# Two attention units ahead of the latent products, one-row products in pairs, the heads' Sqrt behind the last Exp

## The chip, the core and the metric

The program runs on one core of one Trainium2 chip, as one launch. The core has five engines that run their own instruction streams and meet at semaphores: TensorE (PE, matrix products and transposes into eight PSUM banks), VectorE (DVE), ScalarE (ACT), GpSimd (POOL) and SyncE (SP, which here issues the weight loads). The metric is device time in microseconds (us) of one execution.

## The reference, cut to what matters

Two transformer blocks run one after the other on 256 tokens of width 1024, in float32. The first block has attention over 512 keys (256 context, 256 own), of two kinds with four heads each, and a mixture of 32 experts with four chosen per token; the second has a pooling mixer, windowed attention and a wide feed-forward part. The change touches the attention of the first block:

```
mod  = silu(c) @ w_ada + b_ada          # 6 vectors of 1024; sa, sca before attention, ga, sf, scf, gf behind it
q    = rmsnorm(cq, q_norm_w) @ w_uq     # latent queries:  q_nope, q_rope per head
kv   = rmsnorm(ckv, kv_norm_w) @ w_ukv  # latent keys and values: k_nope, mv per head
diff:  p = softmax(q1 k1) - lam * softmax(q2 k2);  o = p @ dv          # 4 heads
mla:   p = softmax(q_nope k_nope + q_rope k_rope); o = p @ mv          # 4 heads
o_diff = rmsnorm(o_diff, subln_w) * 0.8        # per head: needs a square root
x_new  = x + ga * (concat(o_diff, o_mla) @ w_out)
```

## The kernel before, in words

**Weights.** All weights go through a ring of 12 slots of 1 MB in SBUF. SP issues the chunks in a fixed order (`FRONT`: ada0, w_in, w_uq, w_ukv, ada1, ada2, w_out; then 16 pairs of experts in blocks of two slots; then the second block). SP waits with a chunk until PE has counted up `ring_freed` to the chunk's place minus 11, so a slot is loaded again when the products that read it are done.

**Order of the work.** Nothing is scheduled by a program: every engine's stream is written out by hand, and the order of attention comes from one function, `skewed_order`, that PE, ACT and DVE all loop over. There are 16 units, each a head and a half of the queries (128 of them): units 0 to 7 are the differential heads (kind "d", two score tiles each, s{u}_0 and s{u}_1), units 8 to 15 the latent heads (kind "m", one score tile). A unit has four steps, which are skewed by one unit each: *score* (PE multiplies queries and keys, DVE takes the negated maximum of each row, ACT takes Exp with its sum), *mix* (DVE: reciprocal, and for "d" the difference of both softmaxes into `prob`, two buffers), *turn* (PE transposes the probabilities, tile pT{u}, ACT copies them to `probT`) and *value* (PE multiplies with the values, tile av{u}, DVE scales it into `o`).

**Banks.** Every PSUM tile has a name in `FRONT_TILES`, and the tiles take the eight banks in turn, in the list's order. `claim` makes PE wait until the bank's last tile was read, `take` makes a reader wait until the tile is full, `wait_read` waits for a tile's reading. The list has to follow the order in which PE fills the tiles.

**Ahead of attention.** Behind the input projection, PE transposes keys and queries (dkT, dqT) and the latents (cqT, ckvT, krT), multiplies the latent queries with w_uq (qrope, qnope0, qnope1), then w_ukv with the latents: knope0 to knope3 (copied by ACT into knT) and mv0 to mv3 (copied by DVE), and transposes the rotated queries (qrT). These nine tiles are called the latent products here. Only units 8 to 15 read them.

**Inside attention.** Behind value 3 stand the second and third third of the modulation: ada1 and ada2, of 32 products of 32 columns by 512 each; then eight products bc0 to bc7 whose stationary side is one row of `ones`, which spread the modulation's rows over all partitions (`bc`). DVE adds the bias to ada1 and ada2 and copies the eight tiles. Behind value 5 PE transposes 16 pieces of one row of `bc` into *columns*, which POOL later multiplies with the router's weights. Behind value 9 DVE takes eight sums of squares of the heads (`ms_done`) and ACT their root (`root_done`); behind value 12 DVE scales the heads (`sub_done`). PE waits for `sub_done` before mixT0, the first transpose behind attention, and the products with w_out follow.

ACT holds one table of functions at a time. Exp and Sqrt are in different tables (a Copy or a Square needs no change); the compiler puts ACT_TABLE_LOAD ahead of the first of a kind.

Of the kernel before, what the change touches and what calls it, by code (L numbers as in the profile page):

```python
# [9 lines left out]
ALU = mybir.AluOpType  # L10
# [3 lines left out]
P = 128  # L14
# [93 lines left out]
for _c, _n in CHUNK.items():  # L108
# [9 lines left out]
    + ["qrope", "qnope0", "qnope1"] + [f"knope{h}" for h in range(H)] + [f"mv{t}" for t in range(4)] + ["qrT"]  # L118
)
UNITS = [("d", h, t) for h in range(H) for t in range(NT)] + [("m", h, t) for h in range(H) for t in range(NT)]  # L120
# [21 lines left out]

def skewed_order(n_units):

    order = []
    for i in range(n_units + 3):
        for what, u in (("score", i), ("mix", i - 1), ("turn", i - 2), ("value", i - 3)):
            if 0 <= u < n_units:
                order.append((what, u))
    return order  # L150


for _what, _u in skewed_order(len(UNITS)):
    if _what == "score":
        FRONT_TILES += [f"s{_u}_{c}" for c in range(2 if UNITS[_u][0] == "d" else 1)]
    elif _what != "mix":
        FRONT_TILES.append(f"{'pT' if _what == 'turn' else 'av'}{_u}")
    if _what == "value" and _u == 3:
        FRONT_TILES += ["ada1", "ada2"] + [f"bc{n}" for n in range(8)]
    if _what == "value" and _u == 5:  # L160
        FRONT_TILES.append("columns")
# [56 lines left out]
def build(nc, a, out):  # L218
    with ExitStack() as ctx:
# [726 lines left out]
        def _(act):  # L946
# [72 lines left out]
            act.wait_ge(full("proj3_2"), use("proj3_2") + 1)  # L1019
            for h in range(H):  # L1020
                b = take(act, f"knope{h}")
                step(act.activation(knT[:, h, :], b[:], ACT.Copy), tile=f"knope{h}")

            for what, u in skewed_order(len(UNITS)):
                kind, h, t = UNITS[u]
                if what == "score":
# [13 lines left out]
                elif what == "value" and u == 5:  # L1040
# [172 lines left out]
        def _(dve):  # L1213
# [143 lines left out]
            for t in range(4):  # L1357
                b = take(dve, f"mv{t}")
                step(V.tensor_copy(mv[:, t, :], b[:]), tile=f"mv{t}")
            b = take(dve, "qrT")  # L1360
            step(V.tensor_scalar(qrT, b[:].rearrange("p (j t) -> p j t", j=2), MLA_SCALE, None, ALU.mult), tile="qrT")

            for what, u in skewed_order(len(UNITS)):
                kind, h, t = UNITS[u]
                if what == "score":
# [32 lines left out]
                if what == "value" and u == 12:  # L1398
# [261 lines left out]
        def _(pe):  # L1660
# [143 lines left out]
            nk = ("w_ukv", 0)  # L1804
            ring_wait(pe, nk)
            wkv = slot(nk)[:, 0:1024].rearrange("p (h c) -> p h c", h=H)
            wait_read(pe, "ckvT")
            for h in range(H):
                b = claim(pe, f"knope{h}")
                mm(b[:], wkv[:, h, 0:NOPE], ckvT, True, True).then_inc(full(f"knope{h}"), 1)  # L1810
            for t in range(4):
                b = claim(pe, f"mv{t}")
                m = mm(b[:], ckvT[:, t * P:(t + 1) * P], wkv[:, :, NOPE:2 * NOPE], True, True)
                m.then_inc(full(f"mv{t}"), 1)
            pe.wait_ge(full("mv3"), use("mv3") + 1)
            pe.sem_inc(freed, 1)
            wait_read(pe, "qrope")
            b = claim(pe, "qrT")
            for j in range(2):
                for t in range(NT):  # L1820
# [485 lines left out]
```

## Time and profile before

| | |
|---|---|
| time, 3 runs | 1486.64 us median (1486.0 to 1487.38) |
| profiled execution | 1488.94 us, span 1487.1 us |
| busy, of the span | PE 1377.2 us (93%), PE weight loads 741.3 (50%), DVE 505.0 (34%), ACT 309.9 (21%), POOL 46.9 (3%) |
| DMA moved | 500.07 MB, mean 336 GB/s; GB/s by slice of 37.2 us: 389 120 3 387 398 77 157, then 425 to 429, in the slice before 1153 us 423, then 365 266 108 |

The span is the stretch from the first to the last instruction that the profiler records; the execution's own time is 1.8 us more. A busy share is a mean over stages with different limits, so the stretch in question has to be looked at by itself. In the timelines of one engine the bracket behind a row gives how long the engine had been idle and what ended that. A float32 product shows as two records.

### The profile page before, as it was taken

The page shows a single profiled execution, that of the slowest core. Times are in us where ns is not written, and L with a number is a line of the kernel's source. Part 1 is how long each engine was busy: PE and PEld are TensorE (multiplying, and loading weights), DVE is VectorE, ACT ScalarE, POOL GpSimd, SP SyncE. Part 2 cuts the span into 40 slices and gives each one's busy share as a digit, 9 for nine tenths or more (in the row PEclk, how much of TensorE's full clock was granted, in tenths as well). Part 3 has the DMA queues.
Part 4 walks back from the last instruction along what each step waited for, and adds up shares of the span by engine and source line. Part 5 has one row for each costly group of instructions (what it writes and reads, how often), then busy time and mean ns, then how long its engine had stood idle before and what let it go on. Part 6 is the DMA issues. An engine that isn't in the chain of part 4 may idle for free.

```text
span 1487.1 us, 17478 instructions
## 1 busy us (share of the span) xinstructions
PE 1377.2 (93%) x6850; PEld 741.3 (50%) x6850; DVE 505.0 (34%) x896; ACT 309.9 (21%) x451; POOL 46.9 (3%) x74
## 2 busy tenths in 40 slices
PE   5998999999989889899898898898989899999998
PEld 2785455433334324333334343343333487889987
DVE  2746434313113112121131131111311347755566
ACT  3605233201101101011011010010100254544451
POOL 2000000200000000000000000000000201000000
PEclk9999999999999999999999999999999999999999
DMA  9309925999999999999999999999999973565530
GB/s 389 120 3 387 398 77 157 425 429 428 428 428 429 428 429 427 429 428 429 427 429 429 428 428 428 429 428 429 427 428 423 365 266 108 173 196 181 187 142 29
DMA packets 62766, 500.07 MB, mean 336 GB/s; under 512 B 5288, under 2 KB 21960, under 8 KB 34240
## 3 DMA queue, kind: packets, MB, share of 16 engines
q1 hardware_dynamic: 60480, 492.85, 80.4%
q0 software_dynamic: 2032, 6.05, 1.4%
q8 instruction: 31, 0.51, 0.1%
q10 hardware_dynamic: 208, 0.54, 0.1%
q14 instruction: 15, 0.12, 0.0%
HBM read 498.37 MB, written 1.05 MB: 336 GB/s over the span
## 4 chain that ended last, share of the span: by engine, by line
PE 63%; DMA 23%; DVE 9%; issue 3%; SPq 1%; ACT 1%; DVEq 0%; ACTq 0%; PEldq 0%
PE bank L1662 27%; DMA ring<-in_w 20%; PE bank L671 15%; PE bank L724 15%; DMA ring<-in_w_in 2%; PE bank L746 2%; DVE dk L814 1%; DVE mrows L808 1%; DVE dk L810 1%; DVE mrows L818 1%; PE bank L682 1%; PE bank L696 1%; PE bank L734 1%; SPq L546 1%; PE bank L1849 0%
## 5 line engine op out<-in xcount | busy, mean ns | idle before, releaser
L671 PE MATMUL bank<-ring,xn 128*64 128x512 f32 x2048 | 467.9, 610 | 62.2 <-DMA ring<-in_w 62.1
L671 PEld LDWEIGHTS bank<-ring,xn 128*64 128x64 f32 x2048 | 161.1, 140 | 358.0 <-issue 357.2
L724 PE MATMUL bank<-ring,dq 128*64 128x512 f32 x1024 | 226.8, 595 | 0.1
L760 ACT ACTIVATE sq<-mrows 128x512 f32<-128x512 f32 x32 | 20.1, 630 | 802.8 <-DVE mrows L808 802.8
L808 DVE TENSOR_SCALAR mrows<-bank 128x512 f32<-128x512 f32 x32 | 22.0, 687 | 467.3 <-PE bank L671 467.3
L724 PEld LDWEIGHTS bank<-ring,dq 128*64 128x64 f32 x1024 | 71.0, 137 | 136.5 <-issue 136.1
L827 DVE TENSOR_TENSOR dk<-bank,bc 128x512 f32<-128x512 f32 x32 | 22.1, 691 | 236.0 <-PE bank L724 236.0
L501 DVE TENSOR_TENSOR w_lo<-ring,w_hi 128x2048 fp32r<-128x2048 f32 x34 | 77.7, 2291 | 32.8 <-ACT w_hi L496 32.8
L1662 PE MATMUL bank<-x_hi,w_hi 128*128 128x256 f32 x256 | 72.4, 283 | 0.8 <-DVE h_lo L1540 0.8
L1662 PE MATMUL bank<-x_hi,w_lo 128*128 128x256 f32 x256 | 72.4, 283 | 0.0
L1662 PE MATMUL bank<-h_lo,w_hi 128*128 128x256 f32 x256 | 72.4, 283 | 0.0
L496 ACT ACTIVATE w_hi<-ring 128x2048 fp32r<-128x2048 f32 x36 | 68.4, 1907 | 17.2 <-PE bank L1662 17.0
L653 PEld LDWEIGHTS bank<-xn 128*128 128x128 f32 x512 | 58.4, 192 | 14.0 <-issue 14.0
L746 PE MATMUL bank<-dk,xn 128*128 128x512 f32 x128 | 62.3, 620 | 0.0
L653 PE MATMUL bank<-xn 128*128 128x128 f32 x512 | 61.7, 278 | 0.7 <-DVE xn L789 0.7
L1662 PE MATMUL bank<-w_hi,wide_hi 128*128 128x512 f32 x128 | 50.5, 395 | 0.1
L1662 PE MATMUL bank<-w_lo,wide_hi 128*128 128x512 f32 x128 | 50.5, 395 | 0.0
L1662 PEld LDWEIGHTS bank<-x_hi,w_hi 128*128 128x128 f32 x256 | 49.0, 191 | 2.3 <-issue 1.6
L834 DVE TENSOR_TENSOR xc<-xc,bank 128x512 f32<-128x512 f32 x64 | 44.0, 687 | 17.0 <-PE bank L746 17.0
L1662 PEld LDWEIGHTS bank<-h_lo,w_hi 128*128 128x128 f32 x256 | 49.1, 192 | 0.6
L1662 PEld LDWEIGHTS bank<-x_hi,w_lo 128*128 128x128 f32 x256 | 49.0, 192 | 0.0
L1662 PE MATMUL bank<-w_lo,x_hi 128*128 128x512 f32 (+1 forms) x136 | 47.2, 366 | 0.0
(435 smaller groups left out, 1522.1 us busy)
## 6 DMA issues: line engine op xcount, KB each, us to landing
ring<-in_w SPq DMA_DIRECT2D x186, 2048.0 KB, 17.2
ring<-in_w_ff SPq DMA_DIRECT2D x32, 1024.0 KB, 5.5
ring<-in_w_ada SPq DMA_DIRECT2D x24, 1024.0 KB, 16.0
ring<-in_w SPq DMA_DIRECT2D x12, 1024.0 KB, 18.0
ring<-in_w_out SPq DMA_DIRECT2D x8, 1024.0 KB, 10.5
ring<-in_w_in SPq DMA_DIRECT2D x8, 992.0 KB, 26.4
ring<-in_w_in SPq DMA_DIRECT2D x8, 640.0 KB, 15.0
ring<-in_w_ple_gate SPq DMA_DIRECT2D x4, 1024.0 KB, 4.8
```

Source lines behind the costliest of these rows:

```text
L496: act.activation(hi_of(n).bitcast(F32R), slot(chunk)[:, cols], ACT.Copy).then_inc(sem("w_rounded"), 1)
L501: eng.tensor_tensor(w_lo[:, SLOT_OF[chunk], cols].bitcast(F32R), slot(chunk)[:, cols], hi_of(n), ALU.subtract)\
L546: sp.dma_start(dst, src).then_inc(sem(f"landed{SLOT_OF[chunk]}"), 16)
L653: m = pe.matmul(banks[GATHER_BANKS[k // 4]][:, k % 4 * P:(k % 4 + 1) * P], hf[:, t, k * P:(k + 1) * P], sel[:, t, :], start=t == 0, stop=t ...
L671: m = pe.matmul(banks[bank_no][mine(i), :], gathered[:, k, mine(i)], rows_of(at + i, 2)[:, k % 2, q * 512:(q + 1) * 512], start=k == 0, st ...
L724: m = pe.matmul(banks[OUT_BANKS[c]][mine(i), :], actT[:, k, mine(i)], rows_of(8 + 2 * j + i, 4)[:, r, c * 512:(c + 1) * 512], start=k == 0 ...
L746: pe.matmul(banks[MIX_BANKS[c]][:], selgT[:, t * P:(t + 1) * P], out2[:, c * 512:(c + 1) * 512], start=True, stop=True, skip_group_check=T ...
L760: act.activation(sg[:, cols], gs[:, cols], ACT.Sigmoid, scale=ALPHA).then_inc(moe("sigmoid", which), 1)
L808: dve.tensor_scalar(gs[:, cols], banks[GATE_BANKS[half]][:], LIMIT, None, ALU.min)\
L827: dve.tensor_tensor(out2[:, cols], banks[OUT_BANKS[c]][:], gf[:, cols], ALU.mult)\
L834: dve.tensor_tensor(x2[:, t, cols], x2[:, t, cols], banks[MIX_BANKS[c]][:], ALU.add)\
L1662: return pe.matmul(out_, lhsT, rhs, start=first, stop=last, skip_group_check=True)
```

## The change

Three things are moved; no arithmetic of the reference is changed.

1. `skewed_order` starts with score 0, score 1, mix 0, mix 1 and an entry *latent*, at which all three engines do the latent products; then it goes on as before from unit 2. One Exp of a single column is added on ACT between dqT1 and qnope0 (its result is read by nobody), so that the Exp table is loaded there.
2. ada2 goes from behind value 3 to behind value 4, and the eight one-row products go two at a time behind values 5, 6, 7 and 8; columns goes from behind value 5 to behind value 9.
3. ACT's Sqrt goes from behind value 9 to behind value 13, and DVE's scaling of the heads from behind value 12 to behind value 13.

```diff
+LATENT_TILES = [f"knope{h}" for h in range(H)] + [f"mv{t}" for t in range(4)] + ["qrT"]
...
+ADA_AFTER = {3: 1, 4: 2}
+SPREAD_AFTER = {5: (0, 1), 6: (2, 3), 7: (4, 5), 8: (6, 7)}
+
+
 def skewed_order(n_units):
 
-    order = []
-    for i in range(n_units + 3):
+    order = [("score", 0), ("score", 1), ("mix", 0), ("mix", 1), ("latent", 0)]
+    for i in range(2, n_units + 3):
         for what, u in (("score", i), ("mix", i - 1), ("turn", i - 2), ("value", i - 3)):
-            if 0 <= u < n_units:
+            if (2 if what == "mix" else 0) <= u < n_units:
                 order.append((what, u))
...
# ACT
+            step(act.activation(stat[:, 57:58], lam[:, 0:1], ACT.Exp))
             for j in range(2):
                 b = take(act, f"qnope{j}")
...
-                elif what == "value" and u == 9:
+                elif what == "value" and u == 13:
 
                     act.wait_ge(sem("ms_done"), 3)
                     step(act.activation(stat[:, 48:56], stat[:, 40:48], ACT.Sqrt), "root_done")
...
# DVE
-                if what == "value" and u == 12:
+                if what == "value" and u == 13:
                     dve.wait_ge(sem("root_done"), 3)
...
-                if what == "value" and u == 3:
-
+                if what == "value" and u in ADA_AFTER:
+                    i = ADA_AFTER[u]
                     dve.wait_ge(sem("bada_in"), 64)
-                    for i in (1, 2):
-                        b = take(dve, f"ada{i}")
-                        step(V.tensor_tensor(mrows[:, i, :], b[:], mrows[:, i, :], ALU.add), tile=f"ada{i}")
-                    for n in range(8):
+                    b = take(dve, f"ada{i}")
+                    step(V.tensor_tensor(mrows[:, i, :], b[:], mrows[:, i, :], ALU.add), tile=f"ada{i}")
+                if what == "value" and u in SPREAD_AFTER:
+                    for n in SPREAD_AFTER[u]:
                         b = take(dve, f"bc{n}")
...
# PE
-                if what == "value" and u == 3:
-                    ada(1)
-                    ada(2)
-
-                    wait_read(pe, "ada1")
-                    wait_read(pe, "ada2")
-                    for n, (third, q) in enumerate(((1, 0), (1, 1), (1, 2), (1, 3), (2, 0), (2, 1), (2, 2), (2, 3))):
+                if what == "value" and u in ADA_AFTER:
+                    ada(ADA_AFTER[u])
+                if what == "value" and u in SPREAD_AFTER:
+                    for n in SPREAD_AFTER[u]:
+                        third, q = 1 + n // 4, n % 4
+                        wait_read(pe, f"ada{third}")
                         b = claim(pe, f"bc{n}")
                         mm(b[:], ones[32 * q:32 * q + 1, :], mrows[32 * q:32 * q + 1, third, :], True, True)\
                             .then_inc(full(f"bc{n}"), 1)
-                if what == "value" and u == 5:
+                if what == "value" and u == 9:
                     wait_read(pe, "bc5")
```

PE's order behind the latent queries, before. `cq,ring` is qnope, `ckv,ring` knope, `ring,ckv` mv, L1821 qrT, `xc,dqT` the scores of a "d" unit, L1849 a turn, `dv,dq` a value:

```order
L1662 MATMUL bank<-cq,ring 128x256 x8
L1662 MATMUL bank<-ckv,ring 128x512 x4
L1662 MATMUL bank<-ring,ckv 128x512 x4
L1821 MATMUL bank<-ident,xn 128x128 x4
L1662 MATMUL bank<-xc,dqT 128x512 x6
L1849 MATMUL bank<-ident,xn 128x128 x4
L1662 MATMUL bank<-xc,dqT 128x512 x2
L1849 MATMUL bank<-ident,xn 128x128 x4
L1662 MATMUL bank<-dv,dq 128x128 x4
```

and after (L1833 is qrT, L1862 a turn):

```order
L1672 MATMUL bank<-cq,ring 128x256 x8
L1672 MATMUL bank<-xc,dqT 128x512 x4
L1672 MATMUL bank<-ckv,ring 128x512 x4
L1672 MATMUL bank<-ring,ckv 128x512 x4
L1833 MATMUL bank<-ident,xn 128x128 x4
L1672 MATMUL bank<-xc,dqT 128x512 x2
L1862 MATMUL bank<-ident,xn 128x128 x4
L1672 MATMUL bank<-xc,dqT 128x512 x2
L1862 MATMUL bank<-ident,xn 128x128 x4
L1672 MATMUL bank<-dv,dq 128x128 x4
```

The scores of units 0 and 1 (four rows) now stand ahead of the nine latent tiles, and those of unit 2 stay behind them.

PE's order from the first modulation product, before. `ring,cT` is ada1 and ada2, `mrows,ones` the one-row products, `hT,xn` with `kr,xn` the score of an "m" unit, L1874 the columns:

```order
L1662 MATMUL bank<-ring,cT 32x512 x64
L1662 MATMUL bank<-mrows,ones 128x512 x8
L1662 MATMUL bank<-xc,dqT 128x512 x2
L1849 MATMUL bank<-ident,xn 128x128 x4
L1662 MATMUL bank<-dv,dq 128x128 x4
L1662 MATMUL bank<-hT,xn 128x512
L1662 MATMUL bank<-kr,xn 128x512
L1849 MATMUL bank<-ident,xn 128x128 x4
L1662 MATMUL bank<-dv,dq 128x128 x4
L1874 MATMUL bank<-ident,bc 128x1 x16
L1662 MATMUL bank<-hT,xn 128x512
L1662 MATMUL bank<-kr,xn 128x512
```

and after:

```order
L1672 MATMUL bank<-ring,cT 32x512 x32
L1672 MATMUL bank<-xc,dqT 128x512 x2
L1862 MATMUL bank<-ident,xn 128x128 x4
L1672 MATMUL bank<-dv,dq 128x128 x4
L1672 MATMUL bank<-ring,cT 32x512 x32
L1672 MATMUL bank<-hT,xn 128x512
L1672 MATMUL bank<-kr,xn 128x512
L1862 MATMUL bank<-ident,xn 128x128 x4
L1672 MATMUL bank<-dv,dq 128x128 x4
L1672 MATMUL bank<-mrows,ones 128x512 x2
L1672 MATMUL bank<-hT,xn 128x512
L1672 MATMUL bank<-kr,xn 128x512
```

ada2 stands one unit later than ada1, and the one-row products come in pairs, the first behind the turn and value that follow the first "m" score; the columns stand further on, behind value 9.

ACT's order around the head's Sqrt, before. `xn,psum_sum` is an Exp, `dq` a copy of transposed probabilities, `stat` the Sqrt:

```order
L1033 ACTIVATE xn,psum_sum<-bank,psum_sum 128x512
L1039 ACTIVATE dq<-bank 128x512
L1046 ACT_TABLE_LOAD
L1046 ACTIVATE stat<-stat 128x8
L1033 ACT_TABLE_LOAD
L1033 ACTIVATE xn,psum_sum<-bank,psum_sum 128x512
L1039 ACTIVATE dq<-bank 128x512
L1033 ACTIVATE xn,psum_sum<-bank,psum_sum 128x512
L1039 ACTIVATE dq<-bank 128x512
L1033 ACTIVATE xn,psum_sum<-bank,psum_sum 128x512
L1039 ACTIVATE dq<-bank 128x512 x3
```

and after (the same names):

```order
L1043 ACTIVATE xn,psum_sum<-bank,psum_sum 128x512
L1049 ACTIVATE dq<-bank 128x512
L1043 ACTIVATE xn,psum_sum<-bank,psum_sum 128x512
L1049 ACTIVATE dq<-bank 128x512
L1043 ACTIVATE xn,psum_sum<-bank,psum_sum 128x512
L1049 ACTIVATE dq<-bank 128x512 x2
L1056 ACT_TABLE_LOAD
L1056 ACTIVATE stat<-stat 128x8
L1049 ACTIVATE dq<-bank 128x512
L1059 ACTIVATE hT<-bank 128x512 x2
```

The Sqrt is now behind the last Exp and behind the copy for unit 14, with one copy (unit 15) behind it, and no Exp table is loaded behind it.

## Rows read from the trace of the kernel before

**Rows 1.** Page of the profile, the chain that ended last, by engine.
```profile
PE 63%; DMA 23%; DVE 9%; issue 3%; SPq 1%; ACT 1%; DVEq 0%; ACTq 0%; PEldq 0%
```

**Rows 2.** Busy time by stage, all engines; the first line names the columns.
```profile
core 0: us, PE busy (x) PEld busy (x) DVE busy (x) ACT busy (x) POOL busy (x), PEclk, DMA share, GB/s
192.00:200.00 8.00, 6.20 (x31) 3.36 (x28) 3.38 (x13) 5.53 (x9) 0.00 (x0) 1.00 0.01 4
254.00:256.00 2.00, 2.00 (x12) 0.64 (x10) 0.00 (x0) 0.00 (x0) 0.00 (x0) 1.00 0.00 0
400.00:600.00 200.00, 184.12 (x848) 72.56 (x848) 43.13 (x86) 18.20 (x29) 0.00 (x0) 0.99 1.01 428
```

**Rows 3.** Page, DMA issues: KB of each, us from issue to landing.
```profile
ring<-in_w SPq DMA_DIRECT2D x186, 2048.0 KB, 17.2
```

**Rows 4.** Timeline of PE: start us, us, engine line operation, [idle before].
```profile
120.21 3.67 PE L1662 MATMUL bank<-ckv,ring 128*128 128x512 f32 x8 [0.30 <-PE bank L1662]
...
128.18 2.85 PE L1662 MATMUL bank<-xc,dqT 64*128 64x512 f32 x12
134.47 1.12 PE L1849 MATMUL bank<-ident,xn 128*128 128x128 f32 x4 [3.45 <-DVE xn L1386]
```

**Rows 5.** Timeline of DVE, same stretch.
```profile
129.40 2.87 DVE L1368 TENSOR_REDUCE psum_sum<-bank 128x1 f32<-128x512 f32 x4 [0.36 <-PE bank L1662]
...
133.66 0.75 DVE L1386 SCALAR_TENSOR_TENSOR xn<-xn,psum_sum 128x512 f32<-128x512 f32 x1
...
140.77 1.42 DVE L1368 TENSOR_REDUCE psum_sum<-bank 128x1 f32<-128x512 f32 x2
```

**Rows 6.** Timeline of ACT, same stretch.
```profile
118.67 0.60 ACT L1017 ACTIVATE xn<-bank 128x512 f32<-128x512 f32 x1 [4.18 <-PE bank L1662]
...
130.19 1.28 ACT L1033 ACT_TABLE_LOAD   x1 [5.62 <-DVE psum_sum L1368]
131.49 0.69 ACT L1033 ACTIVATE xn<-bank,psum_sum 128x512 f32<-128x512 f32 x1
```

**Rows 7.** Timeline of PE, the modulation products and what follows.
```profile
148.08 7.07 PE L1662 MATMUL bank<-ring,cT 128*32 128x512 f32 x64
155.49 7.07 PE L1662 MATMUL bank<-ring,cT 128*32 128x512 f32 x64 [0.33 <-PE bank L1662]
163.48 2.29 PE L1662 MATMUL bank<-mrows,ones 1*128 1x512 f32 x16 [0.93 <-DVE mrows L1411]
165.70 2.52 PE L1662 MATMUL bank<-xc,dqT 64*128 64x512 f32 x4
...
170.77 1.59 PE L1662 MATMUL bank<-hT,xn 128*128 128x512 f32 x2
...
174.82 1.15 PE L1874 MATMUL bank<-ident,bc 1*128 1x1 f32 x16
```

**Rows 8.** Busy time and granted clock (PEclk) in two stretches.
```profile
166.00:168.00 2.00, 2.00 (x4) 0.65 (x3) 1.90 (x4) 0.00 (x0) 0.00 (x0) 0.50 1.05 418
174.00:176.00 2.00, 2.00 (x25) 1.86 (x24) 1.81 (x5) 1.38 (x3) 1.48 (x7) 1.00 1.04 442
```

**Rows 9.** Timeline of PE, second half of attention.
```profile
179.39 1.02 PE L1662 MATMUL bank<-hT,xn 128*128 128x512 f32 x2
...
192.96 1.02 PE L1662 MATMUL bank<-hT,xn 128*128 128x512 f32 x2
...
198.42 1.02 PE L1662 MATMUL bank<-hT,xn 128*128 128x512 f32 x2
...
206.96 1.91 PE L1888 MATMUL bank<-ident,dk 128*128 128x128 f32 x16
```

**Rows 10.** Timelines of ACT and of DVE, same stretch.
```profile
193.15 1.28 ACT L1046 ACT_TABLE_LOAD   x1 [2.52 <-DVE stat L1397]
...
194.67 1.28 ACT L1033 ACT_TABLE_LOAD   x1
...
202.72 1.42 DVE L1404 TENSOR_TENSOR dk<-dk,stat 128x512 f32<-128x512 f32 x2
```

More of the change, by code:

```diff
@@ L155 @@
         FRONT_TILES += [f"s{_u}_{c}" for c in range(2 if UNITS[_u][0] == "d" else 1)]
+    elif _what == "latent":
+        FRONT_TILES += LATENT_TILES
     elif _what != "mix":
         FRONT_TILES.append(f"{'pT' if _what == 'turn' else 'av'}{_u}")
-    if _what == "value" and _u == 3:
-        FRONT_TILES += ["ada1", "ada2"] + [f"bc{n}" for n in range(8)]
-    if _what == "value" and _u == 5:
+    if _what == "value" and _u in ADA_AFTER:
+        FRONT_TILES.append(f"ada{ADA_AFTER[_u]}")
+    if _what == "value":
+        FRONT_TILES += [f"bc{n}" for n in SPREAD_AFTER.get(_u, ())]
+    if _what == "value" and _u == 9:
         FRONT_TILES.append("columns")
@@ L1018, in _ @@
                                     ACT.Copy, scale=MLA_SCALE), tile=f"qnope{j}")
[L1019 to L1022, printed above, removed]
             for what, u in skewed_order(len(UNITS)):
                 kind, h, t = UNITS[u]
-                if what == "score":
+                if what == "latent":
+                    act.wait_ge(full("proj3_2"), use("proj3_2") + 1)
+                    for n in range(H):
+                        b = take(act, f"knope{n}")
+                        step(act.activation(knT[:, n, :], b[:], ACT.Copy), tile=f"knope{n}")
+                elif what == "score":
                     for c in range(2 if kind == "d" else 1):
@@ L1803, in _, with latent @@
             pe.sem_inc(freed, 1)
[L1804 to L1820, printed above, removed]
-                    m = pe.transpose(b[:, j * T + t * P:j * T + (t + 1) * P], qr[:, t, j * P:(j + 1) * P], ident[:])
-            m.then_inc(full("qrT"), 1)
+            def latent():
+                nk = ("w_ukv", 0)
+                ring_wait(pe, nk)
+                wkv = slot(nk)[:, 0:1024].rearrange("p (h c) -> p h c", h=H)
+                wait_read(pe, "ckvT")
+                for h in range(H):
+                    b = claim(pe, f"knope{h}")
+                    mm(b[:], wkv[:, h, 0:NOPE], ckvT, True, True).then_inc(full(f"knope{h}"), 1)
+                for t in range(4):
+                    b = claim(pe, f"mv{t}")
+                    m = mm(b[:], ckvT[:, t * P:(t + 1) * P], wkv[:, :, NOPE:2 * NOPE], True, True)
+                    m.then_inc(full(f"mv{t}"), 1)
+                pe.wait_ge(full("mv3"), use("mv3") + 1)
+                pe.sem_inc(freed, 1)
+                wait_read(pe, "qrope")
+                b = claim(pe, "qrT")
+                for j in range(2):
+                    for t in range(NT):
+                        m = pe.transpose(b[:, j * T + t * P:j * T + (t + 1) * P], qr[:, t, j * P:(j + 1) * P], ident[:])
+                m.then_inc(full("qrT"), 1)
             for what, u in skewed_order(len(UNITS)):
                 kind, h, t = UNITS[u]
-                if what == "score" and kind == "d":
+                if what == "latent":
+                    latent()
+                elif what == "score" and kind == "d":
                     if u == 0:
```

17 lines of the change are left out of this document (9 added, 8 removed).

## The prediction

> **What bounds the kernel now.** I read the chain that ended last first [rows 1]: TensorE (PE) carries 63% of the span and DMA 23%, so no single engine sets the end everywhere. Next the busy time by stage [rows 2]. From 400 to 600 us the DMA share is 1.01 at 428 GB/s while PE is busy for 184.12 of 200 us: in the mixture-of-experts stage the weight stream is at its limit. In 192:200 and 254:256 the DMA share is 0.01 and 0.00: twice before that stage the stream stands still, because every ring slot is full and PE has not given one back. So the stream's last start, a little before 260 us, is set by PE, and behind it everything has a fixed length. A check on that: the experts' weights are 186 issues of 2048 KB plus twelve halves [rows 3], 402.7 MB, of which 12 slots (12.6 MB) are there when the stream starts; 390 MB at 428 GB/s are 911 us, which from about 259 us ends at about 1170 us, just where the page's GB/s line falls off (423 in the slice that ends at 1153 us, 365 in the next). Each microsecond taken from the front should therefore come off the end, one for one.
>
> All of the change lies in the front, between 113 and 209 us. There PE is the engine on the chain, with holes. The timeline of PE [rows 4, 7, 9] shows these: PE runs the latent products at 120.21, then the scores of three units at 128.18, and then stands idle for 3.45 us until 134.47, when turn 0 may start; its clock is at the lower level (1.2 GHz) behind that. It runs the two modulation products (ada1, ada2) at 148.08 and 155.49 with nothing of attention between them, then eight one-row products at 163.48, and behind these its granted clock is 0.50 (166:168, [rows 8]): the scores of unit 7, two products of 64x512, take 2.52 us where their like takes 1.1. In the second half of attention a unit's rows come every 3.39 us (179.39 to 192.96 are four periods, [rows 9]), PE-bound; then one period is 5.46 (192.96 to 198.42), where ACT loads the Sqrt table and the Exp table again [rows 10].
>
> **Term 1: two units ahead of the latent products.** PE's order changes as the first ordered rows show. Work is the same; what counts is what runs beside what.
> - PE: the scores of units 0 and 1 start at 120.21 instead of 128.18 [rows 4]. Six such products took 2.85 us, so four take 1.9. The latents follow at 122.1 and last as before, 128.18 - 120.21 = 8.0 us, to 130.1.
> - DVE: the first maximum came 1.2 us behind the first score (129.40, [rows 5]); now 121.4. Four maxima take 2.87 us: 124.2.
> - ACT: the Exp table load (1.28 us, [rows 6]) stood behind the first maximum, on the path. It moves in front of qnope0, where ACT had been idle for 4.18 us (the row at 118.67): hidden. The first Exp starts at about 122.15, each takes 0.69 + 0.1 (read of the sum, partly overlapped), four until 125.4. DVE mixes unit 0 from 124.25 to 125.4 (0.75 us for the large one, 1.2 with the two small ones, [rows 5]) and unit 1 to 126.7, all beside PE's latents.
> - Price: DVE's four mv copies and qrT stand before the maxima of unit 2, ACT's four knope copies before its Exp. qrT is full at about 130.2, DVE has copied it (0.7, a pass as wide as a maximum, [rows 5]) at 130.95, and the scores of unit 2 (130.1 to 131.2) are full at 131.2: no wait. The banks that the latents claim are drained 2 us or more before they are needed.
> - Then: turn 0 at 131.1 (its mix is long done), maxima of unit 2 to 132.7, Exp 132.1 to 133.7, copy of pT0 (0.6) to 134.3, value 0 from 134.4 to 135.4, scores of unit 4 to 136.4, and its maximum at 136.5. It stood at 140.77 [rows 5]. From there DVE's cycle of 3.08 us a unit is unchanged. I take 4.2 us: ada1 starts at 143.9, not at 148.08.
> Bounds: not below 1 (the table load alone is 1.28), not above 8.0, the whole latent block. A hole of 1.3 us is left on PE (133.1 to 134.4), shorter than the 1.8 that 192:200 has at full clock [rows 2].
>
> **Term 2: ada2 behind value 4, the one-row products two at a time.** Before, from ada1's start to the first score of unit 8: 170.77 - 148.08 = 22.7 us [rows 7]. Now: ada1 7.1, the wait for its completion 0.3, scores, turn and value of unit-slot 7 at full clock 2.55, ada2 7.1, wait 0.3: 17.35 us. The eight one-row products come later, 0.285 each (2.29 for eight, [rows 7]), 2.3 in all. Saved: 22.7 - 17.35 - 2.3 = 3.1 us. This is the half clock and the wait of 0.93 before the one-row products (163.48 row). DVE's copies of the spread rows (eight, 0.7 each) no longer stand in one block before the maxima of unit 7; two of them a unit make DVE 1.4 + 1.25 = 2.7 us of a PE period of 3.39 + 0.57 = 3.96, so they hide. Bounds: 0 (each pair costs a bank wait of the size of the 0.93) to 5.4 (they vanish in PE's shadow altogether).
> The ring: ada2 is freed later relative to ada1, but starts at 153.8 instead of 155.5, and its chunks land earlier, since ada1 frees the first of them at 144.8, before the stream has run dry. Four blocks of the experts are loaded by about 186 and wait for PE anyway (192:200 has no DMA, [rows 2]), so no load gets late. The load of router_w waits for the second half of unit 7 and comes earlier; the transposed columns (16 one-column transposes, 1.15 us) come later, at about 181, with the small GpSimd products behind them done some 25 us before PE asks.
>
> **Term 3: units 8 to 15.** Before: from unit 8's first score to that of unit 15, 198.42 - 170.77 = 27.65 us [rows 7, 9]. Now seven periods of 3.39 are 23.7, plus 1.1 for the columns: 24.8 (the 2.3 for the one-row products are in term 2). Saved: 2.8, of which 2.07 is the Sqrt hole (5.46 - 3.39) and the rest what was left of the half clock at 170.77. DVE's eight sums of squares (2.9 us) stay behind value 9; the columns now stand beside them on PE. Bounds: 0 to 3.9.
> So unit 15's scores start at 143.9 + 17.35 + 2.3 + 24.8 = 188.3, not 198.42.
>
> **Term 4: the tail.** Before, from there to mixT0: 206.96 - 198.42 = 8.5 us. Now, from that score's start: its probabilities are copied and pT14 copied at +5.1; Sqrt table 1.28 and Sqrt 0.2 on ACT to +6.6; DVE: reciprocal 0.2, two scalings 1.42 [rows 10], done at +8.4; mixT0 at +8.45. pT15 is copied behind the Sqrt, value 15 ends at +8.3, and its reader on DVE stands behind the scalings, at +9.3, before mixT3, which PE reaches at +9.9. Saved: 0.1, between -1.5 and +1.3. One table load fewer stands before the Sqrt of the first residual rows later on, beside PE's output products, worth nothing.
> Here a rule speaks against the change. The rows show the load in 1.28 us from 193.15 and the next load at 194.67, so that the Sqrt and all else between them have 0.24 us [rows 10]. The Trainium skill (ScalarE: Activation LUTs, What ACT_TABLE_LOAD costs) adds a drain of about 1.38 us, 2.66 in all. By the rule the tail would be 1.4 us longer; by the rows there is no such gap, and the sum goes by them.
>
> **Sum.** 4.2 + 3.1 + 2.8 + 0.1 = 10.2 us off the profiled span of 1487.1, whose execution took 1488.94; the median of the runs shown is 1486.64. Applied to the median: 1476.4.
>
> **Rivals.**
> A. Part of it comes back as small waits in the interleaved stretch: engines that ran in blocks now meet at every unit, and each pair of one-row products, each copy before a maximum can cost a bank wait. For: term 1 rests on margins below 1 us on DVE at 130 us. Against: in 3.96 us DVE has 1.2 us free. With term 1 lost entirely: 1480.6.
> B. The end does not follow the front, because the stream or a late GpSimd load decides. Against: the two standstills of [rows 2]. Time: 1486.6.
> C. Slower: TensorE's clock stays at 1.2 GHz through the interleaved stretch. For: the only fall in the stretch came within 2 us of the one-row products (0.50 in 166:168, [rows 8]), and there are now four places with them, between products of 32 columns and half-empty units. Against: 16 one-column transposes at 174.82 ran at 1.00 [rows 7, 8], and both ada took the same 7.07 us. Price: from 151 to 188 us PE has 37 us of work, each microsecond of work done at the lower level takes a second one. It decides once 10.2 us of that work (more than a quarter) runs at the lower level; all of it gives 1486.6 - 10.2 + 37 = 1513, the part behind the first one-row pair alone (27 us) 1503. The Trainium skill (TensorE: Matmul & The Clock Gate, A second HAM failure mode: psum-queue depth-cycling) says that frequent short idles between groups of products make the clock swing to and fro; in 192:200 [rows 2] PE was busy for 6.20 of 8 us, between groups of products, and its granted clock was 1.00, so the trace does not bear it out here.
> D. More than forecast, as the 1.3 us hole closes or term 2 hides wholly: about 1474.
>
> **How the numbers follow.** Forecast 0.64, A 0.18, B 0.06, C 0.05, D 0.07. The forecast's own range, some 2 us around: 1474.4 to 1478.4. For 8 in 10, A's upper part and D have to be in: 1474.0 to 1480.8. Faster by over 0.2% (3 us, about what a measurement can tell from no change): forecast, D and nearly all of A, 0.88; within 0.2%: B and a rest of A, 0.07; slower: C, 0.05.
>
> **What would show it.** Right: the first score about 120 and an Exp right behind its maximum with no table load before it; ada1 at about 144; no half clock behind the one-row pairs, units every 3.4 us, 4 with a pair; no hole of 2 us before unit 15; mixT0 near 197; the experts' first gather near 237.5 instead of 247.9; DMA 1.01 from there as before. Wrong: a PE wait above 2 us between 131 and 137, a granted clock of 0.5 anywhere from 150 to 190, PE waiting for sub_done (the scalings) for more than 1 us, or an expert stage that starts early and ends as before.

## The result, and the profile after

The changed kernel takes 1479.42 us (median of 5 runs, 1478.42 to 1480.64), the kernel before 1486.64 on the same chip (median of 5, 1486.0 to 1488.79). The ratio is 0.9946, with a 95% interval of 0.9935 to 0.9957: it is faster by 7.2 us, 0.54%. Forecast were 10.2 us off, 1476.4, with a range of 1474.0 to 1480.8. The direction and the range hold; 3 us of the gain are missing. The profiled execution took 1480.64 us with a span of 1478.9 (before 1488.94 and 1487.1).

The page's chain that ended last, of the changed kernel, against [rows 1]:
```profile
PE 65%; DMA 22%; DVE 8%; issue 3%; SPq 1%; ACT 1%; DVEq 0%; ACTq 0%; PEldq 0%
```
The mix of limits is as it was. The timeline of PE over the changed stretch (start us, us, engine line operation, [idle before]), against [rows 4, 7, 9]:
```profile
111.68 1.99 PE L1672 MATMUL bank<-ring,cq 128*128 128x256 f32 x8 [0.50 <-DMA ring<-in_w_uq]
...
117.64 1.99 PE L1672 MATMUL bank<-xc,dqT 64*128 64x512 f32 x8 [0.52 <-PE bank L1672]
...
131.92 1.16 PE L1672 MATMUL bank<-dv,dq 128*128 128x128 f32 x8 [1.00 <-ACT dq L1049]
...
141.54 7.07 PE L1672 MATMUL bank<-ring,cT 128*32 128x512 f32 x64
...
159.00 1.10 PE L1672 MATMUL bank<-hT,xn 128*128 128x512 f32 x2 [0.59 <-PE bank L1672]
...
161.57 1.06 PE L1672 MATMUL bank<-dv,dq 128*128 128x128 f32 x8
162.56 1.13 PE L1672 MATMUL bank<-mrows,ones 1*128 1x512 f32 x4
163.62 1.13 PE L1672 MATMUL bank<-hT,xn 128*128 128x512 f32 x2
164.68 1.12 PE L1672 MATMUL bank<-kr,xn 64*128 64x512 f32 x2
...
185.72 1.02 PE L1672 MATMUL bank<-hT,xn 128*128 128x512 f32 x2
186.67 1.12 PE L1672 MATMUL bank<-kr,xn 64*128 64x512 f32 x2
...
188.22 1.06 PE L1672 MATMUL bank<-hT,dq 128*128 128x128 f32 x8
189.11 1.02 PE L1672 MATMUL bank<-hT,xn 128*128 128x512 f32 x2
...
197.53 1.97 PE L1900 MATMUL bank<-ident,dk 128*128 128x128 f32 x16
```
The hole of 3.45 us before turn 0 is gone, and 1.00 is left before value 0. The scores of units 8 and 15 (159.00, 189.11) lie 30.11 us apart, against 27.65 before: four pairs of one-row products and the columns are among them now, where before there were only the columns; a unit with a pair in it (162.56 to 167.21, where the next pair starts) takes 4.65 us, one without 3.39. Busy time and granted clock by stage of the changed kernel, columns as in [rows 2]:
```profile
160.00:170.00 10.00, 10.00 (x43) 4.80 (x42) 6.15 (x12) 2.75 (x6) 0.00 (x0) 1.00 1.03 424
170.00:180.00 10.00, 10.00 (x45) 4.83 (x44) 5.34 (x11) 2.75 (x6) 0.00 (x0) 1.00 1.01 432
180.00:190.00 10.00, 10.00 (x61) 6.14 (x59) 6.31 (x26) 4.14 (x10) 1.52 (x4) 1.00 0.54 224
400.00:600.00 200.00, 183.15 (x839) 71.90 (x840) 42.01 (x84) 14.97 (x24) 0.00 (x0) 0.99 1.01 429
```
PE never waits from 160 to 190 and its clock is at the upper level: where [rows 8] had 0.50, there is no fall. Behind the front all is as before: from the experts' first gather to the last expert product group fed by the ring, 905.19 us (238.61 to 1143.80) against 905.30 (247.89 to 1153.19). Within the scatter, the end follows the front one for one. What comes behind that row is the same in both kernels, yet it took 335.1 us here and 333.9 in the profile of before (333.7 to 335.1 over all profiles below), so the first gather is 9.3 us earlier and the span 8.2 us shorter.

**The clean measure.** In this profile the stretch is entered 2.8 us earlier than in that of before (the first product with w_uq is at 111.68 instead of 114.49), ahead of all that is changed; over the other profiles below it is at 110.8 to 112.2. That difference is the run's, not the change's: e3, whose instructions up to there are those of before, enters at 111.30. So all that follows is counted from that product, the stretch ends at mixT0, and these numbers are differences of starts in each timeline of PE:

| kernel | first score | ada1 | score of unit 8 | of unit 15 | mixT0 |
|---|---|---|---|---|---|
| before | 13.69 | 33.59 | 56.28 | 83.93 | 92.47 |
| changed | 5.96 | 29.86 | 47.32 | 77.43 | 85.85 |
| changed, profiled again | 5.93 | 29.83 | 47.24 | 77.35 | 85.77 |
| e1: units 0 and 1 ahead, alone | 5.93 | 29.83 | 51.74 | 80.52 | 90.61 |
| e2: ada2 and pairs moved, alone | 13.69 | 33.58 | 50.99 | 82.18 | 90.72 |
| e3: Sqrt moved, alone | 13.71 | 34.93 | 56.37 | 82.57 | 90.98 |
| e4: one-row products in fours | 5.93 | 29.82 | 47.24 | 74.87 | 83.28 |
| e5: pairs on one row group | 6.12 | 30.01 | 47.42 | 85.72 | 94.13 |
| e6: one block of eight | 5.93 | 29.83 | 47.24 | 75.97 | 84.38 |
| e7: no early Exp load | 5.96 | 30.21 | 47.62 | 77.73 | 86.14 |
| e8: e4, ada2 beside ada1 | 5.96 | 29.86 | 48.94 | 76.50 | 84.91 |
| e9: Sqrt back | 5.94 | 29.83 | 47.29 | 78.48 | 87.01 |
| e10: e4 again | 5.93 | 29.82 | 47.28 | 74.91 | 83.32 |

The stretch gained 6.6 us, where 10.2 were forecast and 7.2 were timed. It repeats within 0.1 us from one profile to the next in kernels whose clock stays at the upper level (changed: 85.85, 85.77; fours: 83.28, 83.32). Where the clock falls it does not: up to ada1, before, e2 and e3 run the same instructions, and take 33.59, 33.58 and 34.93 us. There is one profile of before, so each gain over it is uncertain by about that much. The timed gains lie from 1.4 us under to 2.4 us over those of the stretch, but for e7's single run, 3.4 under, in which the experts' stage took 907.2 us instead of 905.2 to 905.9.

### The profile page after: what moved, and what is told of

Its sections match the earlier page's. It is cut to its first block, busy times and chain, and to the rows that moved or that the text cites. A ratio compares the mean times of both kernels' runs of the same rounds, so it can differ in the third digit from the quotient of the medians.

```text
span 1478.9 us, 17484 instructions
## 1 busy us (share of the span) xinstructions
PE 1373.2 (93%) x6850; PEld 738.1 (50%) x6850; DVE 505.5 (34%) x896; ACT 307.8 (21%) x450; POOL 47.0 (3%) x74
## 4 chain that ended last, share of the span: by engine, by line
PE 65%; DMA 22%; DVE 8%; issue 3%; SPq 1%; ACT 1%; DVEq 0%; ACTq 0%; PEldq 0%
PE bank L1672 29%; DMA ring<-in_w 20%; PE bank L733 15%; PE bank L680 15%; PE bank L755 3%; DMA ring<-in_w_ada 2%; DVE dk L823 1%; DVE mrows L817 1%; DVE dk L819 1%; DVE mrows L827 1%; PE bank L705 1%; PE bank L743 1%; PE bank L691 1%; SPq L608 0%; PE bank L2026 0%
## 5 line engine op out<-in xcount | busy, mean ns | idle before, releaser
L733 PEld LDWEIGHTS bank<-ring,dq 128*64 128x64 f32 x1024 | 71.1, 137 | 136.5 <-issue 136.0
```

The source lines that it names most:

```text
L733: m = pe.matmul(banks[OUT_BANKS[c]][mine(i), :], actT[:, k, mine(i)], rows_of(8 + 2 * j + i, 4)[:, r, c * 512:(c + 1) * 512], start=k == 0 ...
```

## The experiments

The expectations count the stretch from the no-position query products, which start 1.8 us behind the one that the table counts from (113.51 and 111.68 above), even where their words say "the first product with w_uq". So their 90.7 (before) and 84.0 (changed) are the table's 92.5 and 85.8.

**e1 to e3: each part alone.** e1 keeps the new order of units and the early Exp, and puts the rest back:
```diff
-ADA_AFTER = {3: 1, 4: 2}
-SPREAD_AFTER = {5: (0, 1), 6: (2, 3), 7: (4, 5), 8: (6, 7)}
+ADA_AFTER = {3: (1, 2)}
+SPREAD_AFTER = {3: tuple(range(8))}
```
with the columns behind value 5 and the Sqrt behind value 9 (its scaling behind value 12). One thing of the second part stays in e1 and e3: the first four one-row products wait for ada1's reading alone, where before all eight waited for that of ada2 too. e2 keeps ada2, the pairs and the columns where the change puts them, and takes the order of units, the late Exp load and the Sqrt of before. e3 keeps the Sqrt's new place alone. In e2 and e3:
```diff
-    order = [("score", 0), ("score", 1), ("mix", 0), ("mix", 1), ("latent", 0)]
-    for i in range(2, n_units + 3):
+    order = [("latent", 0)]
+    for i in range(n_units + 3):
```

> Only the first part of the change (scores of units 0 and 1 ahead of the latent products, Exp table loaded early); both modulation products, all eight one-row products, the columns and the Sqrt stand as before. Measure: the stretch from the first product with w_uq to the first transpose behind attention, 90.7 us before, 84.0 in the changed kernel. Theory (the parts add up, and this one is worth what the changed trace shows up to ada1, 3.8 us): 86.9 us, half clock behind the one-row products as before; time 3.8 us under before. Rival (the gain of the first part only shows because the rest is interleaved too): 89 or more.

> Only the second part: ada2 behind value 4, one-row products in pairs behind values 5 to 8, columns behind value 9; latent products and Sqrt as before. Theory (a pair of one-row products costs 1.06 us plus 0.2, not 0.57, so the four pairs give back nearly all that the missing half clock saves): the stretch is 90.0 us, 0.7 under before, and the time is the same. Rival (0.285 us for each, as forecast): 87.1 us, 3.6 under before.

> Only the third part: the heads' Sqrt and their scaling behind value 13; all else as before. Theory: the hole of 2.07 us before unit 15 goes, the tail stays: stretch 88.5 us, 2.1 under before. Rival (the Sqrt's table load now stands on the path in the tail, load and drain 2.66 us): 90 or more, no gain.

Timed against a before of 1487.55: e1 1484.32 (0.9978, 0.9966 to 0.999), e2 1484.92 (0.9981, 0.9972 to 0.999), e3 1484.73 (0.9985, 0.9976 to 0.9994). The three shares, 0.22, 0.19 and 0.15%, add up to 0.56%, the whole to 0.54%. With each share known only to about 0.1%, that is agreement and no more. In the stretch the parts gained 1.86, 1.75 and 1.49 us, 5.1 together, and the whole 6.6. The parts do not simply add up there: e1 and e3 still have falls of the clock, which the whole has not.

In the stretch, e1 missed its 86.9 us (88.8 counted that way, near the rival's 89). It shows term 1 as it was meant, ada1 earlier by 3.76 us, but only 1.86 of them are left at mixT0: unit 8's period is 6.17 us instead of 5.13, and the clock falls twice. The timeline of PE of e1:
```profile
157.23 2.33 PE L1672 MATMUL bank<-mrows,ones 1*128 1x512 f32 x16 [0.33 <-PE bank L1672]
...
161.65 1.91 PE L1672 MATMUL bank<-dv,dq 128*128 128x128 f32 x8
...
191.05 1.30 PE L1672 MATMUL bank<-hT,dq 128*128 128x128 f32 x8 [1.79 <-ACT dq L1049]
192.14 1.92 PE L1672 MATMUL bank<-hT,xn 128*128 128x512 f32 x2
```
and its busy time and clock:
```profile
162.00:164.00 2.00, 2.00 (x9) 1.69 (x8) 1.90 (x4) 0.00 (x0) 0.00 (x0) 0.50 1.03 406
...
192.00:194.00 2.00, 2.00 (x5) 0.49 (x4) 0.35 (x1) 0.44 (x1) 0.00 (x0) 0.50 0.00 0
```
Once behind the block of one-row products, as before, and once more behind the hole of the Sqrt: the 1.79 us of idle at 191.05 are followed by 0.50, and the tail from unit 15's score is 10.09 us instead of 8.54. I had taken a hole of that size as harmless, since before's profile kept 1.00 in 192:200 [rows 2]. Whether a fall follows it is not fixed by the hole alone.

e2 gained 1.75 us in the stretch, over the theory's 0.7 and under the rival's 3.6. The theory left out that the hole before unit 15 would shrink too: that period is 4.47 us instead of 5.46. From ada1 to unit 8's score it saved 5.28 us (22.69 to 17.41), of which unit 15's score (31.19 us behind, before 27.65) gave 3.54 back: as in the changed kernel, the pairs cost more than they were booked at.

e3 gained 1.49 us, of 2.1 expected. The Sqrt hole went whole: the last period is 3.46 us instead of 5.46. It lost 1.34 us before ada1, where the clock is at 0.53 in 134:140 behind the hole before turn 0, but had nearly all of that back by unit 8's score (56.37, before 56.28). Of this, 0.6 us is the shorter wait that e3 shares with e1 (0.33 us instead of the 0.93 in [rows 7]):
```profile
161.05 2.33 PE L1671 MATMUL bank<-mrows,ones 1*128 1x512 f32 x16 [0.33 <-PE bank L1671]
```
So 0.6 us of the 1.86 and of the 1.49 belong to the second part. Behind unit 8's score, what is missing of the 2.1 is that unit's own period, 5.67 us instead of 5.13, with a wait of 1.01 us for DVE in it.

**e4 to e6: how many one-row products in one place, and on which rows.** The code puts product n on row 32 q, with q = n % 4, of `ones` and `mrows`. A row group is here one of the four bands of 32 rows that these rows begin, so a pair stands on two of four row groups. e4 puts four together, e5 makes pairs that share a row group, e6 puts all eight behind value 8:
```diff
-SPREAD_AFTER = {5: (0, 1), 6: (2, 3), 7: (4, 5), 8: (6, 7)}
+SPREAD_AFTER = {6: (0, 1, 2, 3), 8: (4, 5, 6, 7)}             # e4, e10
+SPREAD_AFTER = {5: (0, 4), 6: (1, 5), 7: (2, 6), 8: (3, 7)}   # e5
+SPREAD_AFTER = {8: tuple(range(8))}                           # e6
```
In e5 the columns wait for the four copies that they read (bc2 to bc5).

> The changed kernel with the one-row products in two groups of four (behind values 6 and 8), each group on the four row groups of the array. Theory (products on different row groups run side by side, so four take the 1.06 us that two take): two groups cost 2.5 us instead of four pairs' 5.0, stretch 81.5 us against 84.0, time 2.5 us under the changed kernel. Rival (0.53 us for each product plus the change of kind, however grouped): 83.6 to 84.0. Rival (DVE's four copies in a row, 2.9 us, hold up the next maximum): 82.5 to 84, with a wait of PE before a turn.

> The changed kernel with other pairs: both one-row products of a pair now read the same row group of the array (0 with 4, 1 with 5, 2 with 6, 3 with 7) instead of neighbouring ones. Nothing else moves but the columns' wait. Theory (side by side only on different row groups): a pair takes 2.1 us instead of 1.06, the period of a unit with a pair 5.7 instead of 4.65, the stretch from the qnope products to mixT0 88.2 us instead of 84.0. Rival (a pair's 1.06 us is a fixed cost of changing to one-row products, or a wait for banks): 4.65 and 84.0 as before.

> The changed kernel with all eight one-row products in one block behind value 8, ahead of full units and behind full units. Theory on PE's time: 2.3 us for the block as in the kernel before. Theory on the clock (the half clock in the kernel before came from the one-row block right behind 14 us of 32-column products and a wait of 0.9 us; here it stands among full products): granted clock 1.00 through 150 to 200. Rival (the one-row block alone makes it fall): 0.50 for some us behind it, a loss of 2 to 3 us. DVE's eight copies (5.8 us) hold up the maximum of unit 12, and with it turn 12: a wait of PE of 1 to 3 us. Stretch from the qnope products to mixT0: 83 to 84.5 without the fall, 86 or more with it.

e4: 1477.70 us (before 1487.55; 0.9935, 0.9922 to 0.9949), e6 1479.57 and e5 1487.30 in one run each (before 1486.5). The timeline of PE of e4:
```profile
164.97 1.14 PE L1672 MATMUL bank<-mrows,ones 1*128 1x512 f32 x8
166.04 1.12 PE L1672 MATMUL bank<-hT,xn 128*128 128x512 f32 x2
```
of e5:
```profile
162.24 1.98 PE L1672 MATMUL bank<-mrows,ones 1*128 1x512 f32 x4
164.15 1.12 PE L1672 MATMUL bank<-hT,xn 128*128 128x512 f32 x2
...
175.15 1.91 PE L1672 MATMUL bank<-hT,xn 128*128 128x512 f32 x2
176.99 2.07 PE L1672 MATMUL bank<-kr,xn 64*128 64x512 f32 x2
```
and of e6:
```profile
173.05 2.34 PE L1672 MATMUL bank<-mrows,ones 1*128 1x512 f32 x16
```
Each product is two instructions. Four products (x8) occupy PE from 164.97 to 166.04, 1.07 us; two on different row groups take 1.06 (162.56 to 163.62 in the changed kernel); two on the same row group 1.91 (162.24 to 164.15); eight about 2.3. So what stands on four different row groups runs side by side, and what shares one runs in turn. The Trainium skill (TensorE: Matmul & The Clock Gate, Part 3: Packing small matmuls — row/col tiling, The mechanism) says just that, products at different row groups overlap; the trace agrees with 1.07 us for four. The prediction did not weigh this rule.

e5 brought out something else. Busy time and clock of e5:
```profile
172.00:174.00 2.00, 2.00 (x14) 1.59 (x13) 1.14 (x3) 1.17 (x3) 0.00 (x0) 1.00 1.08 459
174.00:176.00 2.00, 2.00 (x5) 0.53 (x3) 1.37 (x2) 0.20 (x1) 0.00 (x0) 0.84 0.96 410
176.00:178.00 2.00, 2.00 (x3) 0.50 (x2) 0.01 (x1) 0.00 (x0) 0.00 (x0) 0.50 0.96 410
```
With PE busy all the time the clock falls behind the third pair, and stays at 0.50 until 182. Its fourth period is 8.70 us, the ones before it 5.5; the fifth, over which the clock is down once more, 6.24 instead of the changed kernel's 4.66. That makes 4.8 of the 8.3 us that e5's stretch is longer than the changed kernel's; four longer pairs, 0.85 each, make the other 3.4. e6's block of eight, among units in full swing and without a wait before it, left the clock at 1.00 in 170:182. The hold-up by DVE that its expectation names came, but smaller and later: behind the eight copies and the sums of squares, and through ACT, it reaches PE three units further on, before a value:
```profile
187.04 1.16 PE L1672 MATMUL bank<-hT,dq 128*128 128x128 f32 x8 [0.72 <-ACT dq L1049]
```
That period is 4.55 us instead of 3.39, and it makes e6's stretch 1.1 us longer than that of e4, which has no such wait.

**e7: no early Exp load.** One line is taken out:
```diff
-            step(act.activation(stat[:, 57:58], lam[:, 0:1], ACT.Exp))
```

> The changed kernel without the early Exp, so that the table load (1.28 us) stands before the first real Exp again. Theory (the mixes of units 0 and 1 are done 5 us before turn 0 since the latent products stand between, so the load is covered now): ada1 at most 0.5 us later than the 28.0 us behind the qnope products of the changed kernel. Rival (it is on the path, as it was in the kernel before): 1.3 us later.

1483.59 us in one run (before 1486.5), too coarse for this question; the profile answers it. The timeline of ACT of e7:
```profile
120.11 1.28 ACT L1042 ACT_TABLE_LOAD   x1 [1.81 <-DVE psum_sum L1377]
...
130.48 0.69 ACT L1042 ACTIVATE xn<-bank,psum_sum 128x512 f32<-128x512 f32 x1 [3.35 <-DVE psum_sum L1377]
```
and of PE of e7:
```profile
132.75 1.16 PE L1671 MATMUL bank<-dv,dq 128*128 128x128 f32 x8 [1.35 <-ACT dq L1048]
```
The load is back on the chain of unit 0, where unit 0's first Exp waits for it. But the latents lie between units 0 and 1 and unit 2, and the delay has to pass through DVE, for which ACT waits 3.35 us before unit 2's first Exp: DVE mixes units 0 and 1 by 0.9 and 1.3 us later, then copies the latents, and among and behind these copies it had 1.1 us of waits in the changed kernel that are gone here. Its next maxima are 0.35 us later (17.46 us into the stretch instead of 17.11). The timeline of DVE, of the changed kernel and of e7:
```profile
128.79 1.42 DVE L1378 TENSOR_REDUCE psum_sum<-bank 128x1 f32<-128x512 f32 x2 [0.36 <-PE bank L1672]
...
129.62 2.87 DVE L1377 TENSOR_REDUCE psum_sum<-bank 128x1 f32<-128x512 f32 x4
```
PE then waits 1.35 us instead of 1.00. The preload is worth 0.35 us.

**The changed kernel again**, to see how far one profile of it can be trusted:

> The changed kernel once more, beside the next: stretch from the qnope products to mixT0 84.0 us if its clock stays full again, time 7 to 8 us under before.

1481.24 us (5 runs, 1479.29 to 1482.42), before 1486.5: 0.9958, 0.9944 to 0.9971. Its stretch is 85.77 us, as in the first profile, with the clock at 1.00 all through. The intervals of the two ratios overlap; the gain is 5 to 7 us.

**e8 to e10: ada2 back beside ada1, the Sqrt back, fours once more.** e8 is e4 with `ADA_AFTER = {3: (1, 2)}`. e9 is the changed kernel without its third part:
```diff
-                elif what == "value" and u == 13:
-
                     act.wait_ge(sem("ms_done"), 3)       # now behind the copy of columns, value 9
...
-                if what == "value" and u == 13:
+                if what == "value" and u == 12:
                     dve.wait_ge(sem("root_done"), 3)
```

> The kernel with groups of four, but ada1 and ada2 again back to back behind value 3 (14 us of 32-column products on end); the one-row products stay apart behind values 6 and 8. It tells which of the two took the half clock away. Theory (the one-row products in a block right behind the modulation products made it fall; full units now lie between): granted clock 1.00 from 145 to 190, stretch from the qnope products to mixT0 within 0.5 us of the 81.5 of the groups of four. Rival (the 14 us of 32-column products on end are enough, and the fall only shows behind them): 0.50 for some us behind ada2, stretch 83 or more.

> The changed kernel with only the third part undone: Sqrt behind value 9, scaling behind value 12, and so a load of the Sqrt table and one of the Exp table inside the units. Theory (parts add up): the hole before unit 15 is back, stretch 1.1 to 2.1 us longer than the changed kernel's 84.0, so 85.1 to 86.1; another 1.6 where the clock falls in the hole, as it did with the first part alone. Rival (the hole is covered, since the columns now stand beside DVE's sums of squares): 84.0 to 84.4.

> The groups of four once more: stretch 81.4 us again, clock 1.00, time 9 to 10 us under before and some 2 to 3 under the changed kernel.

e8: 1477.52 us (before 1487.49; 0.993, 0.9914 to 0.9946), e9 1481.03 (0.9955, 0.9939 to 0.9971), e10 1478.01 (0.9937, 0.9923 to 0.9951).

e8's stretch missed what was expected by 1.6 us, and not through the clock, which stays at 1.00 behind two modulation products on end. Its timeline of PE names the cause:
```profile
148.87 6.56 PE L1672 MATMUL bank<-ring,cT 128*32 128x512 f32 x56 [0.34 <-PE bank L1672]
156.85 1.06 PE L1672 MATMUL bank<-ring,cT 128*32 128x512 f32 x8 [1.42 <-DMA ring<-in_w_ada]
```
ada2 has caught up with the stream and waits 1.42 us for its last chunk (e1, with the same order there, waits 0.75). Putting unit 7 between the two gives the chunk that time; in the time of the whole kernel (1477.52 to 1477.70 of e4) it does not show.

e9's stretch is 1.16 us longer than the changed kernel's, inside what was expected. The timeline of ACT of e9:
```profile
184.95 1.28 ACT L1054 ACT_TABLE_LOAD   x1 [2.35 <-DVE stat L1405]
186.25 0.21 ACT L1054 ACTIVATE stat<-stat 128x8 f32<-128x8 f32 x1
186.47 1.28 ACT L1043 ACT_TABLE_LOAD   x1
187.77 0.69 ACT L1043 ACTIVATE xn<-bank,psum_sum 128x512 f32<-128x512 f32 x1
```
Two loads cost 2.6 us on ACT and one period of 4.47 us on PE instead of 3.39. e10 repeats e4: 83.32 us in the stretch, 0.9937. Fours are 2.5 us shorter in the stretch than the changed kernel, twice, and 9.5 to 9.9 us under before. It is the stretch that tells them from the changed kernel; the intervals of the timed ratios overlap.

## Why the prediction was right, and where it was not

In the clean measure (the forecast counted from 114.49), what was forecast and what came:

| step | before | forecast | measured |
|---|---|---|---|
| to ada1 (term 1) | 33.6 | 29.4 | 29.86 |
| ada1 to unit 8's score (term 2) | 22.7 | 17.35 | 17.46 |
| unit 8's to unit 15's score (terms 2 and 3) | 27.65 | 2.3 + 24.8 = 27.1 | 30.11 |
| to mixT0 (term 4) | 8.5 | 8.45 | 8.42 |

**Term 1, right but for 0.5 us.** Forecast 4.2, measured 3.73. The first score starts 5.96 us into the stretch, not 5.72, since it waits 0.52 us for a bank where the product that stood there before waited 0.30; that is half of the miss, and the rest are a few tenths among the rows behind it. The timeline of DVE of the changed kernel, against [rows 5]:
```profile
118.84 2.87 DVE L1378 TENSOR_REDUCE psum_sum<-bank 128x1 f32<-128x512 f32 x4 [1.56 <-PE bank L1672]
...
122.20 0.75 DVE L1396 SCALAR_TENSOR_TENSOR xn<-xn,psum_sum 128x512 f32<-128x512 f32 x1
...
134.24 1.42 DVE L1378 TENSOR_REDUCE psum_sum<-bank 128x1 f32<-128x512 f32 x2 [0.70 <-PE bank L1672]
```
and that of ACT, against [rows 6]:
```profile
111.55 1.28 ACT L1021 ACT_TABLE_LOAD   x1
...
119.65 0.69 ACT L1043 ACTIVATE xn<-bank,psum_sum 128x512 f32<-128x512 f32 x1 [1.83 <-DVE psum_sum L1378]
```
Unit 4's maximum comes at 22.6 us of the stretch; forecast was 136.5 - 114.49 = 22.0. Maxima, Exp and mixes of units 0 and 1 lie beside the latents, as the term has it. Wrong was the lower bound, "not below 1 (the table load alone is 1.28)": the load alone is worth 0.35 (e7), as all but that is hidden once the latents lie behind units 0 and 1. The gain comes from the order of the units.

**Term 2, the failed step.** That ada2 behind value 4 removes the wait and the half clock came within 0.1 us (17.46). What failed is the size of "the eight one-row products come later, 0.285 each (2.29 for eight, [rows 7]), 2.3 in all". A row of eight was divided by eight, but the 2.29 us were two groups of four running side by side. A pair costs 1.06 us as four do, and the products around it take 0.2 us more than without it: a score of 128 rows is followed by the next after 1.06 us instead of 0.95 (163.62 and 185.72 in the changed kernel's timeline), and a value by what stands behind it after 0.99 instead of 0.89 (161.57 and 188.22). So a unit with a pair takes 4.65 us, not 3.96, and four pairs cost 5.0, not 2.3: 2.7 of the 3.0 us that are missing between the two scores. The columns in the same way cost 1.27, not 1.1, and one period is 3.50. e4 and e10 confirm it from the other side: two groups of four give back 2.5 us. The Trainium skill (TensorEngine Tiling (Array Packing), Key Properties) says that a change of tiling mode drains the engine; the 0.2 us per pair would fit that, though no run here separates a drain from anything else.

**Term 3, right.** PE-bound periods of 3.39 and no hole before unit 15. But the Sqrt's move in itself is worth 1.1 to 1.2 us (e9), not the 2.07 of [rows 9]: where ada2, the pairs and the columns are moved too, the period with the two loads is 4.47 us (e2, e9), where they stand as before it is 5.46 (before) and 5.54 (e1). So half of that hole went with the second part; of the third part alone, on top of before, the same period fell by the whole 2.0 (3.46, e3). Why the hole is smaller behind the second part was not tested.

**Term 4, right.** The timeline of ACT of the changed kernel, against [rows 10]:
```profile
194.21 1.28 ACT L1056 ACT_TABLE_LOAD   x1
195.51 0.21 ACT L1056 ACTIVATE stat<-stat 128x8 f32<-128x8 f32 x1
195.75 0.60 ACT L1049 ACTIVATE dq<-bank 128x512 f32<-128x512 f32 x1
```
The Sqrt starts 0.02 us behind the end of the load and the next copy 0.03 behind the Sqrt. The further 1.38 us that the Trainium skill (ScalarE: Activation LUTs, What ACT_TABLE_LOAD costs) states are not there, and the tail is 8.42 us, not 1.4 longer.

**The rivals.** A's time, 1480.6, is nearer to the 1479.42 than the forecast's, but its mechanism is not what happened: PE does not wait once between 160 and 190. It was occupied longer, not held up. C's "only fall in the stretch" was not the only one: the clock also fell behind the hole before turn 0, as the prediction itself says further up. B fell: 905.19 against 905.30 us for the experts' stage. C's time did not come, and neither did the clock's fall in the changed kernel, but the mechanism exists (e5), with PE busy throughout; in a kernel one edit away it cost 4.8 us. D fell with term 2. The term's lower bound, 0 us, covered the true value (0.2 us: 5.2 saved less 5.0 for the pairs). That the whole range held is in part luck: its upper part was there for rival A's waits, and what filled it was another cause.

**What stays open.** What makes the clock fall. Behind the hole of 3.45 us before turn 0 it fell in before, e2 and e3, for longer in e3 (0.53 in 134:140) than in before:
```profile
134.00:136.00 2.00, 1.53 (x6) 1.20 (x8) 1.90 (x4) 1.00 (x3) 0.00 (x0) 0.59 1.00 410
136.00:138.00 2.00, 2.00 (x7) 0.50 (x6) 1.34 (x4) 1.86 (x5) 0.00 (x0) 0.56 1.02 426
```
It fell behind the block of eight right behind the modulation products (before, e1, e3), behind the Sqrt hole in e1 (a wait of 1.79 us) but not in before (about the same) or in e9 (0.81), and behind three pairs on one row group (e5); it did not behind the same block among full units (e6), nor behind two modulation products without the block (e8). So neither the block, nor the modulation products, nor a hole of 1.8 us is enough by itself, and the same instructions can fare differently from one profile to the next.

## What to carry to other kernels

Take the price of an instruction that you split off a group from how the group runs, not from its time divided by its count: products on different row groups run side by side, and two cost what four cost. Small products of this kind are best dealt out in whole groups of four. Before moving a table load, follow its delay through the engines that read the result: what waits they already have soaks it up (here all but 0.35 us of 1.28). Where a stream behind the front is at its limit, measure the front alone, from a point ahead of the change to one behind it: with a steady clock it repeated within 0.1 us where whole runs scatter by 2. Where the clock falls inside the measured part, take more than one profile, of the kernel before too: the same instructions differed there by 1.3 us. And when a part is put back for an experiment, put back its waits too, or their gain (here 0.6 us) goes to the wrong part.

## What the runs showed of the hardware

- One-row products of 512 columns (f32, two instructions each): two on different row groups 1.06 us, four on four groups 1.07, two on the same group 1.91, eight 2.3.
- The products on either side of such a group took 0.1 us more each: 0.99 instead of 0.89 and 1.06 instead of 0.95 (changed kernel).
- Behind each ACT_TABLE_LOAD of 1.28 us the next instruction started within 0.02 us (changed kernel, 195.51; e9, 186.25 and 187.77).
- The granted clock fell to 0.50 with PE busy for 2.00 of 2 us in e5 (176:178), with no wait of PE for 15 us before it.
- After a hole of 1.8 us the clock held 1.00 in one kernel (before) and fell to 0.50 in another (e1).
- The same instructions up to ada1 took 33.59, 33.58 and 34.93 us in before, e2 and e3, with the clock down for longer in e3.
